# Two transformer blocks in one kernel: x turned in halves ahead of the last matmuls, and the FFN's inverse root applied to its up result

## What is computed

```python
x = x + einsum('bsm,md->bsd', mixed, w_out)
h = rms_norm(x, ffn_norm_w)                    # x * rsqrt(mean(x*x) + eps) * w
u = einsum('bsd,df->bsf', h, w_up)             # 1024 -> 2 * 2816
u = conv_b + sum(conv_w[j] * pad(u)[:, j:j + S] for j in range(3))
x = x + einsum('bsf,fd->bsd', silu(u[gate]) * u[val], w_down)
x = rms_norm(x, final_norm_w)
# block 2: h = rms_norm_2(x, norm1_g); proj = h @ w_in; ...; x = x + y @ w_out
# h = rms_norm_2(x, norm2_g); x = x + relu(h @ w_ff_up)**2 @ w_ff_down; rms_norm
```

## Time and profile before

| | us |
|---|---|
| time, median of 3 runs | 912.42 (912.4 to 914.1) |
| span of the profiled execution | 909.2 |
| PE busy | 863.9 (95%) |
| PEld busy | 771.1 (85%) |
| DVE busy | 570.4 (63%) |
| ACT busy | 468.3 (52%) |
| POOL busy | 38.9 (4%) |
| chain that ended last | PE 81%, DVE 8%, ACT 4%, POOL 3% |

### The profile page before, as it was taken

One profiled execution on the slowest core, in us unless ns is written; L12 is line 12 of the kernel. 1 busy time (PEld: TensorE's weight loads), 2 busy tenths in 40 slices (PEclk: granted clock), 3 DMA queues, 4 the chain that ended last, 5 costly groups with the idle time before them and its releaser, 6 DMA issues.

```text
span 909.2 us, 13342 instructions
## 1 busy us (share of the span) xinstructions
PE 863.9 (95%) x5272; PEld 771.1 (85%) x5272; DVE 570.4 (63%) x807; ACT 468.3 (52%) x681; POOL 38.9 (4%) x100
## 2 busy tenths in 40 slices
PE   6989897999999999998999999999999999999998
PEld 5777786999999987887778788999899799999996
DVE  5894656676676778247787863456566655555554
ACT  5653553655555546357656645544474544444441
POOL 0000100000000000002321210100000000000000
PEclk9999697999999999799999999999999999999999
DMA  9543112555555574544444445232235455555551
GB/s 347 197 149 130 46 48 96 164 195 194 182 184 188 185 232 121 186 154 133 159 158 139 143 153 168 69 118 70 89 121 178 146 185 186 185 185 185 185 185 46
DMA packets 89133, 140.54 MB, mean 155 GB/s; under 512 B 3568, under 2 KB 56176, under 8 KB 88960
## 3 DMA queue, kind: packets, MB, share of 16 engines
q1 hardware_dynamic: 88944, 139.79, 46.4%
q10 hardware_dynamic: 144, 0.13, 0.0%
...
HBM read 138.86 MB, written 1.05 MB: 154 GB/s over the span
## 4 chain that ended last, share of the span: by engine, by line
PE 81%; DVE 8%; ACT 4%; POOL 3%; issue 2%; DMA 1%; SPq 0%; DVEq 0%; ACTq 0%
PE bank L445 24%; PE bank L446 23%; PE bank L447 23%; PE bank L337 3%; PE bank L802 2%; PE bank L828 2%; DVE w_lo L1266 2%; ACT w_hi L925 2%; PE bank L762 1%; DVE arena L1612 1%; POOL heads_newton L433 1%; DMA raw<-in_w_in 1%; DVE h_lo L1300 1%; POOL heads_newton L437 1%; POOL heads_newton L434 1%
## 5 line engine op out<-in xcount | busy, mean ns | idle before, releaser
L1266 DVE TENSOR_TENSOR w_lo<-raw,w_hi 128x1024 fp32r<-128x1024 f32 (+2 forms) x260 | 306.8, 1205 | 126.9 <-ACT w_hi L925 126.9
L925 ACT CAST w_hi<-raw 128x1024 fp32r<-128x1024 f32 (+2 forms) x260 | 262.7, 1035 | 177.2 <-PE bank L447 168.9
L445 PE MATMUL bank<-h_hi,w_hi 128*128 128x256 f32 x736 | 211.4, 287 | 2.7 <-DVE h_lo L1300 2.7
L446 PE MATMUL bank<-h_lo,w_hi 128*128 128x256 f32 x736 | 209.8, 285 | 0.0
L447 PE MATMUL bank<-h_hi,w_lo 128*128 128x256 f32 x736 | 209.7, 285 | 0.0
L445 PE MATMUL bank<-w_hi,h_hi 128*128 128x512 f32 (+2 forms) x368 | 145.2, 395 | 8.1 <-DVE w_lo L1266 3.5
L445 PEld LDWEIGHTS bank<-h_hi,w_hi 128*128 128x128 f32 x736 | 142.8, 194 | 4.4 <-issue 3.2
L446 PEld LDWEIGHTS bank<-h_lo,w_hi 128*128 128x128 f32 x736 | 142.8, 194 | 0.9
L446 PE MATMUL bank<-w_lo,h_hi 128*128 128x512 f32 (+2 forms) x368 | 143.0, 388 | 0.0
L447 PE MATMUL bank<-w_hi,h_lo 128*128 128x512 f32 (+2 forms) x368 | 142.9, 388 | 0.0
L447 PEld LDWEIGHTS bank<-h_hi,w_lo 128*128 128x128 f32 x736 | 142.7, 194 | 0.0
...
## 6 DMA issues: line engine op xcount, KB each, us to landing
...
```

The source lines that it names most:

```text
L445: nc.tensor.matmul(dst, l_hi, r_hi, start=start, stop=False)
L446: nc.tensor.matmul(dst, l_hi, r_lo, start=False, stop=False)
L925: nc.scalar.copy(dst, raw_half(m % RAW, half, size, cols)).then_inc(s.hi_done, 1)
L1266: nc.vector.tensor_tensor(dst, raw_half(n // 2 % RAW, n % 2, size, cols), h, ALU.subtract).then_inc(s.lo_done, 1)
```

## The change

x is turned in two halves of its columns: "low" (tiles 0 to 3) and "high" (4 to 7).

- w_out of block 1 to FFN1: the low turns stand between tile 0 and tile 1 of the last matmuls. `scale_x` is gone and x is turned unscaled. FFN1's first two weight halves are begun on the low tiles (`first_columns`, `column_part`), into banks 0 and 3, and finished on the high ones. The inverse roots, one for each token, are made into a row over all partitions by two matmuls with the identity (`ffn_row`), and a new DVE multiplication, `scale_up`, takes every 512-column up result from PSUM times that row into SBUF (`up_rows`), 22 times in all. `taps` and `convolve` read `up_rows`; they and PE's bank reuse wait for `up_scaled`. In DVE's list of a chunk: scale gate, lo of two, convolve gate, scale value, convolve value, lo of two, and the rest as before.
- FFN1 to block 2: the last down matmuls go by column half and token tile (`last_columns`), the low turns stand ahead of the last quarter; x is added in four parts; the projection's first two weight halves run ahead of the high turns. ACT's hi of halves n2 + 2 and 3 moves between the low and the high eviction, DVE's ahead of the high h_lo.
- w_out of block 2 to FFN2: low turns ahead of the last two weight halves, FFN2 begun on the low tiles; ACT's hi of FFN2's second slab moves behind the high tiles.

```diff
+        up_rows = area(4096, 2, 2, 512)
+        ffn_row = area(8192, TOKENS)
...
+            def last_columns(n, lhs, accs, between):
+
+
+                pe.wait_ge(s.lo_done, n + 2)
+                for b in range(2):
+                    for a in range(TT):
+                        acc, c0, c1 = accs[a][b]
+                        between(b, a)
+                        for e in range(2):
+                            q = (n + e) % RING
+                            ins = passes(acc, lhs[0][:, e, a * P:(a + 1) * P], lhs[1][:, e, a * P:(a + 1) * P],
+                                         w_hi[:, q, c0:c1], w_lo[:, q, c0:c1], False, e == 1)
+                        if b == a == 1:
+                            ins.then_inc(s.mm_done, 2)
+                        else:
+                            ins.then_inc(s.tile_done, 1)
+
...
+            def column_part(n, ks, dst, lhs):
+
+                q = n % RING
+                pe.wait_ge(s.lo_done, n + 1)
+                for k in ks:
+                    wh, wl = w_hi[:, q, k * P:(k + 1) * P], w_lo[:, q, k * P:(k + 1) * P]
+                    ins = passes(dst, wh, wl, lhs[0][:, k, :], lhs[1][:, k, :], k == 0, k == KT - 1)
+                return ins
...
+            def turn_part(a, ks, banks=(4, 5, 6, 7)):
+
+                for k in ks:
+                    ins = turn(bank[:, banks[k // 2], k % 2 * TOKENS + a * P:k % 2 * TOKENS + (a + 1) * P],
+                               x[:, a, k * P:(k + 1) * P])
+                    if a == 1 and k % 2 == 1:
+                        ins.then_inc(s.x_turned, 1)
+
+            LOW, HIGH = range(4), range(4, KT)
...
-            for c in range(2):
-                chunk_rows(26 + 2 * c, C_OUT + c, 512, al,
-                           lambda k: pe.wait_ge(s.mixed_lo, k // 2 + 1) if k % 2 == 0 else None,
-                           halves=(2, 3) if c == 0 else LAST)
-
-
-            turn_x(xn, lambda a: pe.wait_ge(s.x_scaled, a + 1))
-            ready = h_ready(1)
-
-            def ff1_up(n, e, i=None, j0=None, ready=None):
+            chunk_rows(26, C_OUT, 512, al, lambda k: pe.wait_ge(s.mixed_lo, k // 2 + 1) if k % 2 == 0 else None,
+                       halves=(2, 3))
+            low = [(pair(C_OUT + 1, 512)[:, a], 0, 512) for a in range(TT)]
+            pe.wait_ge(s.lo_done, 32)
+            for a in range(TT):
+                for e in range(2):
+                    q = (30 + e) % RING
+                    for k in range(2):
+                        t, at = 4 + 2 * e + k, k * 512
+                        ins = passes(low[a][0], al[0][:, t, a * P:(a + 1) * P], al[1][:, t, a * P:(a + 1) * P],
+                                     w_hi[:, q, at:at + 512], w_lo[:, q, at:at + 512], False, e == k == 1)
+                ins.then_inc((s.tile_done, s.mm_done)[a], a + 1)
+                if a == 0:
+                    pe.wait_ge(s.acc_free1, 5)
+                    turn_part(0, LOW)
+                    turn_part(1, LOW)
+
+
+            def ff1_up(n, e, i=None, j0=None):
 
                 for v in range(2):
                     if i is not None or j0 >= 2:
-                        pe.wait_ge((s.gate_conv, s.val_conv)[v], j0 - 1 if i is None else i * 2 + j0 - 1)
+                        pe.wait_ge(s.up_scaled, 2 * j0 - 3 + v if i is None else i * 4 + 2 * j0 - 3 + v)
                     for f in range(2):
-                        half_columns(n + 2 * v + f, KT, 1, bank[:, 2 * e + v, f * TOKENS:(f + 1) * TOKENS], h, i,
-                                     ready if v == f == 0 else None)
+                        half_columns(n + 2 * v + f, KT, 1, bank[:, 2 * e + v, f * TOKENS:(f + 1) * TOKENS], h, i)
+
+            def first_columns(n, dsts, norm, tile0, tile1):
+
+
+                tile0()
+                turn_part(0, HIGH)
+                pe.wait_ge(s.h_lo_done, 4 * norm + 2)
+                column_part(n, LOW, dsts[0], h)
+                tile1()
+                turn_part(1, HIGH)
+                column_part(n + 1, LOW, dsts[1], h)
+                pe.wait_ge(s.h_lo_done, 4 * norm + 4)
+                for f in range(2):
+                    column_part(n + f, HIGH, dsts[f], h).then_inc(s.mm_done, 1)
...
-            pe.wait_ge(s.acc_free0, 6)
-            ff1_up(n1, 0, None, 0, ready)
-            pe.wait_ge(s.acc_free1, 5)
+            first_columns(n1, (bank[:, 0, 0:TOKENS], bank[:, 3, 0:TOKENS]), 1, lambda: pe.wait_ge(s.x_tiles, 1),
+                          lambda: pe.wait_ge(s.acc_free0, 6))
+            for f in range(2):
+                half_columns(n1 + 2 + f, KT, 1, bank[:, 1, f * TOKENS:(f + 1) * TOKENS], h)
+            pe.wait_ge(s.ffn_rms, 1)
+            for a in range(TT):
+                ins = nc.tensor.matmul(bank[:, 4, a * P:(a + 1) * P], st[:, 2 + a:3 + a].to_broadcast([P, P]), ident[:],
+                                       start=True, stop=True)
+            ins.then_inc(s.ffn_row, 1)
...
+            def low_turned(b, a):
+
+                if b == a == 1:
+                    pe.wait_ge(s.x_tiles, 3)
+                    turn_part(0, LOW, IN2_BANKS)
+                    turn_part(1, LOW, IN2_BANKS)
+
             pe.wait_ge(s.act_lo_done, CH1)
-            last_halves(2 * M_IN2 - 2, 1024, (0, 1), 1, al, down_banks)
+            last_columns(2 * M_IN2 - 2, al, down_banks, low_turned)
 
 
             n2 = 2 * M_IN2
-            pe.wait_ge(s.val_conv, CH1)
-            turn_x(x, lambda a: pe.wait_ge(s.x_tiles, 2 + a), IN2_BANKS)
             ready = h_ready(2)
-            chunk_rows(n2, C_GLA, 512, h, ready)
+            chunk_rows(n2, C_GLA, 512, h, ready, (0, 1))
+            pe.wait_ge(s.x_tiles, 5)
+            turn_part(0, HIGH, IN2_BANKS)
+            turn_part(1, HIGH, IN2_BANKS)
+            chunk_rows(n2, C_GLA, 512, h, ready, (2, 3))
             chunk_rows(n2 + 4, C_GLA + 1, 512, h)
             chunk_rows(n2 + 8, C_GLA + 2, 16, h, halves=(0, 1), kn=4)
...
+                    pe.wait_ge(s.acc_free1, 18)
+                    turn_part(0, LOW)
+                    turn_part(1, LOW)
...
-            ff2_up(n3, 0, 0, None, ready)
+            first_columns(n3, (bank[:, 2, 0:TOKENS], bank[:, 3, 0:TOKENS]), 3, lambda: pe.wait_ge(s.x_tiles, 6),
+                          lambda: pe.wait_ge(s.acc_free0, 19))
...
+            half_squares(0, 0)
+            turned_hi(h_hi, 0, 4, s.x_turned, 4, lambda k: column("ffn_norm_w", k), s.h_hi_done)
+            half_squares(0, 1)
+            act.wait_ge(s.x_tiles, 1)
+            half_squares(1, 0)
+            act.wait_ge(s.acc_free0, 6)
+            half_squares(1, 1).then_inc(s.ssq, 1)
+            turned_hi(h_hi, 0, KT, s.x_turned, 4, lambda k: column("ffn_norm_w", k), s.h_hi_done, first=4)
             hi(34, 35)
...
 
-            def ff1_chunk(j, e, mm, split1, split2, split3):
-
-                act.wait_ge(s.mm_done, mm)
+            def ff1_chunk(j, e, split1, split2, split3):
+
+                act.wait_ge(s.up_scaled, 2 * j + 1)
                 taps(j, e, 0)
                 split1()
-                act.wait_ge(s.mm_done, mm + 2)
...
+            turned_hi(h_hi, 0, 4, s.x_turned, 8, lambda k: column("norm1_g_2", k), s.h_hi_done, IN2_BANKS)
             hi(n2 + 2, n2 + 3)
-
-
-            turned_hi(h_hi, 0, KT, s.x_turned, 8, lambda k: column("norm1_g_2", k), s.h_hi_done, IN2_BANKS)
...
-            hi(*range(n + 16, n + 24))
-            turned_hi(h_hi, 0, KT, s.x_turned, 12, lambda k: column("norm2_g_2", k), s.h_hi_done)
+            hi(*range(n + 16, n + 22))
+            turned_hi(h_hi, 0, 4, s.x_turned, 12, lambda k: column("norm2_g_2", k), s.h_hi_done)
+            turned_hi(h_hi, 0, KT, s.x_turned, 12, lambda k: column("norm2_g_2", k), s.h_hi_done, first=4)
...
-            lo(32, 33)
+            lo(32)
             add_chunk(C_OUT, C_OUT, 30)
+            lo(33)
+            turned_lo(h_lo, h_hi, 0, 4, s.h_hi_done, 4, lambda k: column("ffn_norm_w", k), s.h_lo_done)
...
+            turned_lo(h_lo, h_hi, 0, KT, s.h_hi_done, 4, lambda k: column("ffn_norm_w", k), s.h_lo_done, first=4)
             dve.wait_ge(s.ssq, 3)
             link(nc.vector.tensor_tensor(st[:, 2:4], st[:, 0:2], st[:, 10:12], ALU.add))
-            inverse_root(st[:, 2:4])
-            scale_x(0)
-            scale_x(1)
-            turned_lo(h_lo, h_hi, 0, KT, s.h_hi_done, 4, lambda k: column("ffn_norm_w", k), s.h_lo_done)
+            inverse_root(st[:, 2:4], None, s.ffn_rms, 1)
             lo(34, 35)
+            dve.wait_ge(s.ffn_row, 1)
+            link(nc.vector.tensor_copy(ffn_row, bank[:, 4, 0:TOKENS]))
 
...
+            def scale_up(j, e, v, mm, src=None):
+
+                dve.wait_ge(s.mm_done, mm)
+                src = bank[:, 2 * e + v, :].rearrange("p (f t) -> p f t", f=2) if src is None else src
+                nc.vector.tensor_tensor(up_rows[:, v, e, :].rearrange("p (f t) -> p f t", f=2), src,
+                                        ffn_row.rearrange("p (o t) -> p o t", o=1).to_broadcast([P, 2, TOKENS]),
```

(28 more changed lines are left out.)

70 lines of the change are left out of this document (32 added, 38 removed).

## The result

The changed kernel takes 930.39 us (median of 4 runs, 929.38 to 931.04), the kernel before 912.41 beside it: a ratio of 1.0195, 95% interval 1.0179 to 1.0211. It is slower by 18.0 us; 14.0 were predicted, with a range of 919 to 932. The profiled execution took 930.32 us with a span of 928.5. The kernel before has a span of 909.2 in its trace. The spans of the two traces are thus 19.3 us apart and the medians 18.0.

A forecast was written before the change was run, and what follows sets the result against it. TensorE, busy 863.9 of 909.2 us, bounds the kernel; VectorE's queue order decides its FFN1 waits. +3.7 + 9.0 + 1.7 + 2.2 - 2.6 = +14.0 gives a span of 923.2, plus 3.2 a median of 926.4 us; range 919 to 932.

The forecast's parts named there:

- A and first chunks: w_out to FFN1's third up: a gain of 2.15 us turns into a loss of 3.7 (bounds 2.2 to 5.5).
- eight chunks of the loop: FFN1 chunks 2 to 9: TensorE waits 1.13 us for a weight split in each, 9.0 in all (7.4 to 11.0).
- last chunk up to the last down matmuls: End of FFN1: scales and convolution behind the splits make 13.1 us into 14.8, a loss of 1.7.
- junction B: FFN1 to block 2: TensorE waits 2.4 us for a split behind root and scaling; loss 2.2 (bounds 1.2 to 3).
- junction C: w_out of block 2 to FFN2: one wait of 1.05 us, no clock fall; gain 2.6 (bounds 0.8 to 3.2).
- 5.76 for an up pair: FFN1 loop: 48 up matmuls take 5.76 us at full clock, added to 12.36 for a chunk of 18.1.
- the chain: FFN1 loop: VectorE and ScalarE steps in queue order after the first up pair, ending with the needed split at 12.3 us.
- sentence on the Trainium skill: FFN1 loop: by the skill's fixed terms SBUF reads would save some 0.35 us a chunk, the 9.0 nearing 6.
- Rival 2: FFN1 loop late by under 0.5 us a chunk, from quicker starts between engines or SBUF operands: 920.6 us; chance 0.10.
- Rival 1: FFN1 loop: added scaling hidden in VectorE's 5 us of idle, so the kernel is faster: 908.7 us; chance 0.07.
- rival 3: Slower still: TensorE's waits bring the clock to 1.2 GHz for stretches of the loop, 931 to 934 us; chance 0.13.
- that fall (1.9 us): Start of FFN1 in the kernel before: granted clock 0.50 makes the first 20 matmuls cost 1.9 us more.

The follow-up runs named there:

- experiment on the taps: Changed kernel with ScalarE's tap of chunks 1 to 10 reading TensorE's bank again instead of the copy in SBUF; 930.04 us, ratio 1.0201.
- C alone: Kernel before with only the change's w_out-to-FFN2 part (low turns ahead of the last matmuls, FFN2 begun on the low tiles); 910.24 us, ratio 0.9973.
- B alone: Kernel before with only the change's FFN1-to-block-2 part (last down matmuls by columns, block 2 begun on tiles 0 to 3); 916.03 us, ratio 1.0034.
- B mended: Changed kernel with ScalarE's and VectorE's next splits moved ahead of mean_squares and the roots at FFN1 to block 2; 927.96 us, ratio 1.0151.
- the first chunk mended: Changed kernel with, in FFN1's first chunk only, row of roots and first split earlier, first multiplication cut in two; 921.56 us, ratio 1.0090.
- scale_first: Changed kernel with one line moved in VectorE's FFN1 chunk: the value's scale_up ahead of the gate's convolution; 918.47 us, ratio 1.0059.
- dosed, reordered kernel: Changed kernel with all reorderings (loop, first chunk, FFN1 to block 2, last chunk), plus each value multiplication made twice; 914.79 us, ratio 1.0032.
- dose_after: Changed kernel, its order kept, with the value's multiplication by the roots made twice in each of 11 chunks; 936.78 us, ratio 1.0267.

## Why the prediction was right, and where its terms were off

| stretch (TensorE's marks) | predicted, us | traced, us |
|---|---|---|
| ahead of w_out's end | 0 | +3.1 |
| w_out's end to the third up (A and first chunks) | +3.7 | +3.9 |
| eight chunks of the loop | +9.0 | +9.5 |
| last chunk up to the last down matmuls | +1.7 | +1.9 |
| junction B | +2.2 | +4.2 |
| block 2 | 0 | -0.7 |
| junction C | -2.6 | -2.65 |
| sum | +14.0 | +19.3 |

**Loop.** Right in mechanism and, to 0.05 us, in each step of the queue. Counted from the end of the first up pair (214.46, where the value half's first matmul starts), VectorE's rows above stand at 3.12, 5.40, 7.21, 9.30 and 11.12; 3.1, 5.4, 7.2, 9.3 and 11.1 were predicted. TensorE needs the split at 225.46 + 0.23 = 225.69 and starts at 226.85, 1.16 late where 1.13 was predicted. The chunk is 1.27 longer all the same. The term that was short is the 5.76 for an up pair: behind a wait its second matmul starts 0.22 us after the first (208.60, 208.82) and not 0.12, and the pair takes 5.86. The eight chunks sum to 9.5 and not 10.2 because the last one waits 0.41 only.

A tap takes longer from SBUF than was put down (1.09 the pair; 1.05 and 1.0 stood in the chain), but the starts behind a release came 0.15 to 0.17 us after it and not 0.2, and the two nearly cancel. That the sum of the chain came out so near is in part luck. The experiment on the taps shows that they are worth 0.15 us a chunk; they aren't what the prediction missed, although its period of 18.1 and the 18.10 of that kernel look alike. VectorE's reads from SBUF cost the same as from a bank, 479 ns, as the prediction took them from the earlier trace rows. Its sentence on the Trainium skill ("VectorE: DVE Perf Modes", "The TRN2 errata") can be closed with this: ScalarE's reads differ in the sense of its figures, 594 against 560 ns, somewhat less than the 43 ns estimated from them, and VectorE's, 479 to 480 against 479, don't. Rival 2 (under 0.5 us a chunk) is out by the same rows.

**Rival 1** (the work is hidden) was wrong for this order and right for another one: with 12.98 to 12.99 us of VectorE's work in a chunk both orders do the same, and one takes 18.25 us, the other 16.98. That the earlier trace rows showed 5 us of idle VectorE time told nothing about which of the two it would be; its queue did.

**Junction A and the first chunks.** The wait of 4.65 behind the row of roots (4.5 predicted) and the one of 2.28 ahead of the third up (2.6 predicted) are there, the low clock behind the first one too. The prediction had 1.8 of waiting inside the second up; there is none, the low clock fills its place, as it had said. It laid the 2.6 to VectorE's late start in chunk 0, and there it was wrong. The runs show two causes: with the row of roots and the splits ahead, the 4.65 and its low clock go and 7.6 us come back, but the wait ahead of the third up stays at 2.28; with the loop's order altered the 4.65 stays and the 2.28 goes.

**Junction B.** The wait of 2.19 for w_lo and its cause (mean_squares and the root ahead of the split) are as predicted: the mended order removes it. The other 1.9 us are the last down matmuls at a granted clock of 0.63, 18 of them at 0.329 instead of 0.23 us, behind the tail's wait of 3.52. The prediction had the tail's length right (+1.7) and did not ask what clock it would leave behind: the sum has no term for it. That is rival 3's mechanism, at this one place; the fall behind the 4.65 took the place of a wait.

**Block 2.** The -0.7 is two stretches of low clock that lie elsewhere in the two traces. In the kernel before the granted clock is 0.68 from 369.5 to 377.2 (the 48 matmuls of 16 columns at the end of the projection, 0.158 us apart) and 0.61 from 377.2 to 384; in the changed one the same matmuls have 0.99 (0.110 us apart) and then 0.74. That gives back 3.1 us right behind junction B. From 676 to 680 the changed kernel has 0.50, where the kernel before has 1.00, and loses 2.4. Whether the change has a part in either isn't shown: C alone has the first stretch as the kernel before (0.159 us apart), B alone has 0.116, and the second stretch is in the traces with B mended and with the first chunk mended, but not in those of B alone and C alone.

**Junction C.** -2.65 against -2.6, and 2.5 us faster in the runs of C alone: no clock fall, one wait of 0.97.

**Ahead of w_out's end** the code is the same. The 3.1 us there are in the trace of C alone as well, whose code is unchanged up to FFN2: attention's half-clock stretch comes later in both. The same mark (the transposes that start at 129.01 in the kernel before and at 132.11 in these two) lies at 128.77 with the first chunk mended and at 134.70 in scale_first. The windows of the kernel before and then of C alone:

```profile
102.00:111.00 9.00, 8.18 (x35) 7.48 (x33) 6.64 (x15) 3.75 (x11) 3.49 (x12) 0.50 0.00 1
111.00:120.00 9.00, 8.45 (x51) 7.46 (x50) 5.71 (x17) 5.28 (x19) 0.00 (x0) 0.90 0.01 2
```

```profile
102.00:111.00 9.00, 6.07 (x38) 5.50 (x37) 6.63 (x15) 3.75 (x11) 3.50 (x12) 0.88 0.00 0
111.00:120.00 9.00, 8.38 (x32) 7.25 (x32) 6.24 (x17) 4.60 (x17) 0.00 (x0) 0.50 0.01 3
...
156.00:160.00 4.00, 3.99 (x32) 3.98 (x33) 4.00 (x8) 1.14 (x4) 0.00 (x0) 1.00 0.00 0
```

C alone then starts FFN1 at full clock (last row), where the kernel before ran at 0.50; its third up comes at 184.70, so 1.8 of the 3.1 us are given back. What the prediction did was to credit junction A with removing that fall (1.9 us), read from one execution's trace; in the trace of C alone, with the same junction A, it isn't there. Against C alone, which is alike ahead of w_out's end, the first chunks cost 190.38 - 184.70 = 5.7 us. With this the 18.0 us close: 14.0, and 2.0 for the first chunks, 0.5 for the loop, 0.2 for the tail, 2.0 for the clock in B, less 0.7 in block 2. That is a sum over single traces, whose low-clock stretches alone move by 2 to 3 us; that it meets the medians to 0.1 is luck. So is part of the prediction's hit: its range holds 930.39, but near the upper end, by stretches of low clock that its sum put at nothing or credited to A.

What stays open: why the clock falls behind some waits and not behind others. Behind each wait of FFN1 from 2.48 us up (2.48, 2.90, 2.97, 3.08, 3.38, 3.52, 3.66, 4.12, 4.65) it fell; behind 1.7 to 1.8 never. Between these it went both ways: it fell behind 2.00 at the old junction C, behind 2.24 in B alone and behind 2.20 ahead of the third up with the taps from the bank, and it stayed up behind 2.28 ahead of the third up and behind 2.37 ahead of the first down matmuls of the dosed, reordered kernel. At one and the same place, the w_lo wait in block 2, it stayed up behind 2.19 in the changed kernel and fell behind 2.20 in dose_after and 2.22 with the taps from the bank. In the projection of the kernel before it fell with no wait at all (369.5 to 384). So the length of a wait between 2.0 and 2.4 us doesn't decide it. No run was made to settle what does.
